# Two transformer blocks on one core: routing by token tiles with two more weight slots, a reordered second mixer, and a final norm by tiles

## The chip, the cores and the metric

The kernel runs on 1 core of one Trainium2 chip. The metric is device time in microseconds (us) for one execution; the figure for a kernel is the median of several. All data are float32. The program is written for each engine by hand: TensorE (PE) multiplies matrices into eight banks of PSUM (128 partitions x 512 floats each), VectorE (DVE), ScalarE (ACT) and GpSimd (POOL) compute on SBUF and PSUM, SyncE (SP) issues nearly all DMA loads. Engines wait for one another on semaphores only.

## The reference

256 tokens of width 1024 pass through two blocks.

```python
# block 1
h = rms_norm(x, norm1_w) @ w_in
x = x + concat(dilated_attention(q, k, v), hgrn2(...)) @ w_out
h = rms_norm(x, norm2_w)
affinity = softmax(h @ w_router)               # 16 experts
# each expert takes the 32 tokens with its highest affinity
x = x + sum over experts of affinity * down(silu(gate(h_e)) * up(h_e))   # 1024 -> 1024 -> 1024
# block 2
proj = x @ w_in_2
merged = (sigmoid(g0) * (rwkv7(...) @ w_up_rwkv) + sigmoid(g1) * (attention(q, k, v) @ w_up_moba)
          + sigmoid(g2) * (s5_with_glu(u) @ w_up_ssm))
x = layer_norm(1.189 * x + merged @ w_out_2, ln1_w, ln1_b)
x = layer_norm(1.189 * x + moe(x), ln2_w, ln2_b)  # 32 experts of 256, two for each token
```

Block 1's expert weights are 16 x 3 matrices of 4 MB: 201 MB of the 375 MB that the kernel moves. hgrn2 is a gated recurrence in both directions, s5 a state space scan, rwkv7 a recurrence with a 64 x 64 state for each of 8 heads.

## The kernel before

The work is cut into stages, each with a program for each engine. On an engine stages follow one another in the order in which the last lines of the kernel call them; where two stages alternate, a string names whose turn it is (`take_turns`, line 151), each letter being one step up to the next `yield`. A step of `project` (line 410) is half a job: 8 products of 128 x 128 by 128 x 512, or their equal.

**Slots.** Weights pass through a ring of six slots of 2 MB (`slot_number`, line 314). SyncE may load into a slot when the counter `units_used`, which TensorE raises, says that its last content has been read. For block 2 three of the slots remain (0 to 2), and the other three hold activations.

**Routing of block 1.** `out_proj1` multiplies the mixer's output by w_out, four jobs (two column halves, within each two token tiles), and VectorE adds each to x. Then, for both tiles together: `norm2` (ScalarE squares the rows, lines 349 to 362), `turn2` (TensorE turns h, line 375, VectorE copies it with norm2_w, line 388), the router's logits (line 883), softmax, the search for the 32 best of each expert (lines 936 to 942, VectorE, 16 partitions), the one-hot matrix `chosen` (line 945), and the gather of all 16 experts' tokens as a product with `chosen` (line 900), 512 columns wide. The affinities times `chosen` are turned too (lines 906, 911), for the sum over experts at the end.

**Experts of block 1.** `experts1` is a hardware loop of 4 rounds over 4 experts. An expert's inputs and the affinities are first copied by VectorE into fixed places, since the loop's matmuls need fixed addresses. Gate and up (line 1015) are products with 32 columns of weights loaded into the array, for two column strips (n = 0, 1) in turn; then hidden rows are turned (1024), multiplied by down (1035), and every four experts are added to x (1049). SyncE issues the 96 loads of 2 MB at line 998. Beside the experts, ScalarE loads the tables of the state space scan, and GpSimd works on them; both begin when the gather is over.

**Mixer of block 2.** The scan (`ssm`, line 1249) has 8 groups: drive (TensorE, line 1277), rotation and scan (VectorE, 1325 to 1336), products (GpSimd, 1364 to 1367), emit (TensorE, 1290: 8 products of 32 output columns, which take turns by output tile). TensorE alternates it with the projection for rwkv7. Then come two steps of the attention's projection, the GLU projection, and the recurrence, which alternates with the attention's and the gates' projection: this one has a single PSUM bank (7), which ScalarE must copy out (line 1245) before the next job. ScalarE also issues the loads for the recurrence (lines 1459 to 1461). The recurrence inverts matrices in doubling rounds (1563), then passes through four chunks (1592 to 1608), one after the other. After it come the rest of the gates' projections alternating with the attention, and only then `merge` (1786): for each of 8 tiles of the width the three branches' products, then VectorE's gates and sums. The output weights are the next thing in the ring, and `load_ln_rows` asks for the second router's vectors and weights when the merge is over.

**End.** The 32 experts of block 2 accumulate into four PSUM banks, which four products with zeros have opened. Then VectorE adds 1.189 x over the whole width (line 2361), `layer_norm` (1825 to 1856) goes over both tiles at once, and one store of 1 MB follows (line 2371).

## Time and profile before

| | |
|---|---|
| median of 3 runs | 1559.55 us (1558.82 to 1563.98) |
| the profiled execution | 1559.29 us, its span in the trace 1557.5 us |
| mean granted TensorE clock | 0.924 |
| TensorE busy | 1328.4 us, 85% |
| VectorE, ScalarE, GpSimd busy | 28%, 13%, 8% |
| DMA | 375.39 MB, mean 241 GB/s |

The stages by TensorE's time: block 1's projections, attention and hgrn2 to 224, output projection to 254, norm and routing to 299, its experts to 762, projection and scan to 877, GLU and the recurrence's front to 1036, its chunks to 1080, gates and attention to 1175, merge to 1220, output projection and routing 2 to 1295, experts of block 2 to 1537, norm and store to 1557. In a row of the windows, the count in brackets is the number of instructions, PEclk is the granted TensorE clock as a share of full speed, and the DMA share is that of 16 engines. Each product in the code shows as two matmul instructions in the trace.

### The profile page before, as it was taken

To read this page: it belongs to the slowest core of one execution; us is meant where nothing else is said; L and a number is where in the kernel's file an instruction comes from. 1 tells how busy PE (TensorE), PEld (TensorE's weight loads), DVE (VectorE), ACT (ScalarE), POOL (GpSimd) and SP (SyncE) were. 2 spreads that over 40 slices of the span, in tenths; PEclk is the share of its full clock that TensorE was granted. 3 is DMA by queue.
4 is the path that set the end of the run, shared out by engine and by line. 5 is a ranking of instruction groups with operands and counts; after the bars stand their busy time and mean duration, and the time that the engine had idled before them with its cause. 6 is when DMAs were issued, how large, how long until landed. Compare 5 with 4: busy or idle time off the path is not lost.

```text
span 1557.5 us, 16762 instructions
## 1 busy us (share of the span) xinstructions
PE 1328.4 (85%) x6962; PEld 678.7 (44%) x6962; DVE 440.7 (28%) x850; ACT 205.6 (13%) x372; POOL 118.1 (8%) x146
## 2 busy tenths in 40 slices
PE   6999257798997998988889888978999779999994
PEld 3574244332322322322534545867767544334341
DVE  3242752300100100100156337433442251111113
ACT  2022311000000000000000012101123013112111
POOL 0000000388000000000043200000000000000000
PEclk9999568899999999999999999995998979999998
DMA  9533102299999999999621353110230664999990
GB/s 351 210 109 113 51 0 108 86 424 428 428 427 430 427 428 430 428 428 430 243 79 57 108 189 109 56 56 1 109 108 0 251 246 174 422 421 422 421 403 28
DMA packets 62361, 375.39 MB, mean 241 GB/s; under 512 B 6112, under 2 KB 7392, under 8 KB 37472
## 3 DMA queue, kind: packets, MB, share of 16 engines
q1 hardware_dynamic: 58816, 367.87, 58.1%
q10 hardware_dynamic: 3488, 6.72, 1.2%
q8 instruction: 41, 0.67, 0.2%
q14 instruction: 16, 0.13, 0.0%
HBM read 373.53 MB, written 1.05 MB: 240 GB/s over the span
## 4 chain that ended last, share of the span: by engine, by line
PE 65%; DMA 20%; DVE 9%; ACT 3%; issue 2%; POOL 1%; SPq 0%; ACTq 0%; POOLq 0%; DVEq 0%; PEldq 0%
DMA arena<-in_w_expert_up 15%; PE psum L435 11%; PE psum L438 10%; PE psum L1015 8%; PE psum L2237 6%; DMA arena<-in_expert_w_up 3%; PE psum L1035 3%; PE psum L2261 3%; PE psum L1786 3%; PE psum L2272 2%; PE psum L1563 2%; PE psum L1888 2%; PE psum L1290 2%; PE psum L1024 1%; DVE arena L762 1%
## 5 line engine op out<-in xcount | busy, mean ns | idle before, releaser
L1015 PE MATMUL psum<-arena 128*32 128x512 f32 x1024 | 239.9, 598 | 28.8 <-DMA arena<-in_w_expert_up 22.3
L435 PE MATMUL psum<-arena 128*128 128x512 f32 x416 | 189.7, 608 | 9.5 <-ACT arena L1245 4.7
L438 PE MATMUL psum<-arena 128*128 128x256 f32 x736 | 168.2, 384 | 5.0 <-DVE arena L386 1.6
L438 PEld LDWEIGHTS psum<-arena 128*128 128x128 f32 x736 | 138.5, 191 | 30.9 <-issue 8.3
L1015 PEld LDWEIGHTS psum<-arena 128*32 128x32 f32 x1024 | 62.6, 110 | 194.4 <-issue 140.8
L1035 PE MATMUL psum<-arena 128*32 128x512 f32 x512 | 133.0, 680 | 7.6 <-ACT arena L1059 7.6
L435 PEld LDWEIGHTS psum<-arena 128*128 128x128 f32 x416 | 78.5, 194 | 108.1 <-issue 106.9
L2237 PE MATMUL psum<-arena 128*64 128x512 f32 x512 | 116.1, 595 | 1.7 <-DMA arena<-in_expert_w_up 1.4
L1077 DVE TENSOR_TENSOR arena<-arena,psum 64x512 f32<-64x512 f32 x16 | 10.9, 680 | 251.6 <-ACT arena L1057 251.6
L1035 PEld LDWEIGHTS psum<-arena 128*32 128x32 f32 x512 | 31.7, 123 | 95.9 <-issue 85.4
L2237 PEld LDWEIGHTS psum<-arena 128*64 128x64 f32 x512 | 38.2, 137 | 66.5 <-issue 66.0
L2272 PE MATMUL psum<-arena 128*128 128x512 f32 x128 | 59.3, 605 | 0.9 <-DVE arena L2348 0.9
L2261 PE MATMUL psum<-arena 128*64 128x512 f32 x256 | 57.9, 592 | 0.8 <-ACT arena L2305 0.8
L1179 POOL TENSOR_TENSOR arena<-arena 128x16 f32<-128x16 f32 (+6 forms) x64 | 43.9, 687 | 24.0 <-DMA arena<-in_ssm_bc 19.1
L1024 PE MATMUL psum<-arena 64*128 64x64 f32 x128 | 33.3, 401 | 13.6 <-DVE arena L1080 13.6
L1786 PE MATMUL psum<-arena 128*128 128x256 f32 x192 | 44.0, 394 | 0.6 <-DVE arena L607 0.6
L1364 POOL TENSOR_TENSOR arena<-arena 128x512 f32<-128x512 f32 x8 | 10.1, 1266 | 448.8 <-DVE arena L1336 405.8
L1080 DVE TENSOR_TENSOR arena<-arena,psum 64x512 f32<-64x512 f32 x16 | 10.9, 680 | 116.4 <-PE psum L1015 116.4
L1024 PEld LDWEIGHTS psum<-arena 64*128 64x128 f32 x128 | 31.0, 324 | 28.2 <-DVE arena L1080 28.2
L1786 PEld LDWEIGHTS psum<-arena 128*128 128x128 f32 x192 | 38.1, 199 | 6.9 <-issue 1.4
L1057 ACT ACTIVATE arena<-psum 64x512 f32<-64x512 f32 x16 | 9.5, 591 | 226.0 <-PE psum L1015 226.0
L2272 PEld LDWEIGHTS psum<-arena 128*128 128x128 f32 x128 | 23.0, 189 | 37.0 <-issue 35.3
(450 smaller groups left out, 1303.3 us busy)
## 6 DMA issues: line engine op xcount, KB each, us to landing
arena<-in_w_expert_gate SPq DMA_DIRECT2D x32, 2048.0 KB, 23.2
arena<-in_w_expert_up SPq DMA_DIRECT2D x32, 2048.0 KB, 24.1
arena<-in_w_expert_down SPq DMA_DIRECT2D x32, 2048.0 KB, 21.8
arena<-in_w_in SPq DMA_DIRECT2D x21, 2048.0 KB, 11.6
arena<-in_expert_w_gate SPq DMA_DIRECT2D x32, 1024.0 KB, 11.5
arena<-in_expert_w_up SPq DMA_DIRECT2D x32, 1024.0 KB, 13.6
arena<-in_expert_w_down SPq DMA_DIRECT2D x32, 1024.0 KB, 10.2
arena<-in_w_out SPq DMA_DIRECT2D x4, 2048.0 KB, 8.4
```

The lines of the kernel that those rows point to most:

```text
L435: mm = pe.matmul(o, lhs[:, k, sub * P:(sub + 1) * P], w[:, k, :], start=(k == 0), stop=(k == kt - 1))
L438: mm = pe.matmul(o, w[:, k, c:c + P], lhs[:, k, :], start=(k == 0), stop=(k == kt - 1))
L1015: mm = pe.matmul(ps[32 * n:32 * n + 32], xcur[:, k], w, start=(k == 0), stop=(k == KD - 1))
L1024: mm = pe.matmul(turned_ps[:, 64 * c:64 * c + 64], by_four[:, c], ident[0:64, 0:64], start=True, stop=True)
L1035: mm = pe.matmul(y_ps[at:at + 32, 512 * n:512 * n + 512], hid_T4[:, j, half], w_slot(e4, 4 + half)[:, j, 512 * n:512 * n + 512], start=(ha ...
L1179: mul = lambda o, a, b: step(pool.tensor_tensor(o, a, b, ALU.mult))
L1290: mm = pe.matmul(o, c[:, 32 * tile:32 * tile + 32], pr[:, n, i * SEQ:(i + 1) * SEQ], start=(n == 0), stop=(n == 3))
L1563: mm = pe.matmul(bank(b0 + t)[R, g * 64:(g + 1) * 64], lhs[R, t, g], rhs[R, t, g], start=True, stop=True)
L1786: mm = pe.matmul(o, w[:, k, d * P:(d + 1) * P], y[:, k], start=(k == 0), stop=(k == 3))
L2237: mm = pe.matmul(in_ps[ROOM * h:ROOM * (h + 1)].rearrange("p (j n) -> p j n", j=2), tokens[u % 2][:, k, ROOM * h:ROOM * (h + 1)], w_in[2 * ...
L2261: mm = pe.matmul(y_ps[ROOM * h:ROOM * (h + 1), 512 * n:512 * (n + 1)], turned[u % 2][:, f * P + ROOM * h:f * P + ROOM * (h + 1)], w_down[2 ...
L2272: mm = pe.matmul(bank(2 * t + n), turned[u % 2][:, (2 + t) * P:(3 + t) * P], y_sb[:, 512 * n:512 * (n + 1)], start=False, stop=not follows)
```

## The change

There are four parts.

1. **Routing by token tiles, two more slots.** One stage, `out_and_route`, takes the place of `out_proj1`, `norm2`, `turn2` and `route`. The output projection goes by token tile. Raw x is turned instead of the normed rows: VectorE multiplies the router's weights by norm2_w once, and the root mean square comes in as the scale of the exponential. Only the tokens of the first four experts are gathered before the experts start; the gather of the other twelve stands in experts 0 to 2, turning of the affinities in expert 3, from where on the tables' load and GpSimd's work begin. Slots 6 and 7 take up two of the first eight loads of expert weights, once; then six are used as before. The experts' loop is written out, and the copies to fixed places are gone.
2. **Block 2's mixer reordered.** Emit goes through both tiles at each of its four steps. The orders are new: two projection steps more ahead of the first emit, three projection steps instead of two ahead of the GLU, single steps in the gaps of the doubling rounds and of the chunks (which are now cut into three). The products of k and v in a chunk go ahead of the state's. ScalarE applies the gates' sigmoid as it copies out the bank. All gate projections use bank 7. The merge goes by branch, 12 jobs, and alternates with the attention; its weights come in the order ssm, rwkv, attention, each slot being free after its four jobs. ScalarE copies q and k of the attention and y of the recurrence. Block 2's slots are 3 to 5.
3. **Final norm by tiles** (`Finish`). 1.189 times the identity in place of the zeros puts 1.189 x into the banks. The statistics are taken from PSUM by tile with bn_stats, the rest goes by half rows, with four stores of 256 KB.
4. **Block 2's norm and experts.** `load_ln_rows` and the output projection wait for 4 double tiles instead of 8 tiles, and the experts' first two loads change places.

```diff
+        E1_SLOTS = [4, 5, 0, 1, 2, 3, 6, 7]
...
+                project_out(0, 0, range(KD))
+                project_out(0, 1, range(KD))
+                project_out(1, 0, range(4))
+                turn(0, 0)
+                turn(0, 1)
+                project_out(1, 0, range(4, KD))
+                route(0, range(KD))
+                project_out(1, 1, range(6))
+                turn(1, 0)
+                project_out(1, 1, range(6, KD))
+                route(1, range(2))
+                pe.wait_ge(*count("o1_product", 4))
+                pe.sem_inc(inc("units_used"), 1)
+                turn(1, 1)
+                route(1, range(2, 4))
+                route(1, range(4, KD))
...
+                for half in range(2):
+                    for j in range(4):
+                        gather(pe, 4 * half + j, bank(2 + half)[:, j * P:(j + 1) * P], slice(0, first))
...
+            beside = {0: range(0, 3), 1: range(3, 6), 2: range(6, KD)}
...
+                        before = [v for v in range(u) if slot_number(v) == slot_number(u)]
+                        if before:
+                            sp.wait_ge(*count("units_used", before[-1] + 1))
...
-                    for i in range(2):
-                        tile = 2 * s + i
-                        o = bank(4 + q % 2)[32 * (tile % 4):32 * (tile % 4) + 32, 0:SEQ]
-                        for n, c in enumerate((c_re, nc_re, nc_im, nc_im)):
+                    for n, c in enumerate((c_re, nc_re, nc_im, nc_im)):
+                        for i in range(2):
+                            tile = 2 * s + i
+                            o = bank(4 + q % 2)[32 * (tile % 4):32 * (tile % 4) + 32, 0:SEQ]
...
+            branches = ((2, ycT, ("glu_out", 1)), (0, yaT, ("rw_out", 2)), (1, ybT, ("mb_out", 4)))
+            jobs = [(place, b, y, ready, j) for place, (b, y, ready) in enumerate(branches) for j in range(KD // 2)]
...
-            act.wait_ge(*count("mg_T", KD))
+            act.wait_ge(*count("mg_T", KD // 2))
...
+                    for n in range(2):
+                        c = slice(512 * n, 512 * n + 512)
+                        dve.scalar_tensor_tensor(x_sb[:, t, c], bank(2 * t + n), self.mean_var[t][:, 0:1], ln_rows["ln2_w"][:, c],
+                                                 ALU.subtract, ALU.mult).then_inc(inc("l2_scaled"), 1)
...
-            take_turns(pe, "b" + "ab" * 16, proj_rkv.parts[0], ssm_scan.parts[0])
...
+            take_turns(pe, "baaba" + "ab" * 14, a=proj_rkv.parts[0], b=ssm_scan.parts[0])
+
+            for _ in range(3):
+                next(beside_rwkv)
             glu_proj.tensor(pe)
-            take_turns(pe, "aaaaabaaabaaaabaabaabababb" + "baaaa", lambda pe: beside_rwkv, rwkv7.parts[0])
-            take_turns(pe, ORDER2[0], proj_gates.parts[0], attention2.parts[0])
-            merged.tensor(pe)
+            take_turns(pe, "gggggr" + "gggr" + "ggggr" + "gr" * 5 + "r" + "gr" * 11 + "ggggg" + "t" + "mm" + "t" + "r" + "tm" * 14,
+                       g=lambda pe: beside_rwkv, r=rwkv7.parts[0], t=attention2.parts[0], m=merged.parts[0])
...
+            take_turns(dve, "mt" * 8 + "t", m=merged.parts[1], t=attention2.parts[1])
```

## Rows read from the trace of the kernel before

**Rows 1.** Windows: us, busy (instructions) of PE PEld DVE ACT POOL, PEclk, DMA, GB/s

```profile
19.00:63.00 44.00, 43.47 (x96) 18.95 (x96) 8.99 (x43) 1.93 (x5) 0.00 (x0) 1.00 0.85 313
...
270.00:279.00 9.00, 0.99 (x4) 0.39 (x4) 7.09 (x20) 0.26 (x3) 0.00 (x0) 0.50 0.00 0
...
299.00:762.00 463.00, 409.63 (x1702) 129.99 (x1703) 39.30 (x72) 24.41 (x40) 74.15 (x106) 0.95 1.00 422
780.00:877.00 97.00, 86.29 (x327) 41.12 (x327) 53.99 (x84) 4.18 (x7) 40.35 (x32) 0.95 0.29 98
1036.00:1080.00 44.00, 34.10 (x538) 32.20 (x534) 11.39 (x25) 4.14 (x7) 0.00 (x0) 0.67 0.01 2
1080.00:1221.00 141.00, 131.34 (x573) 103.79 (x572) 57.66 (x92) 30.37 (x74) 0.00 (x0) 0.92 0.17 60
1153.00:1175.00 22.00, 16.81 (x55) 8.50 (x54) 10.12 (x19) 9.79 (x25) 0.00 (x0) 0.73 0.26 95
```

**Rows 2.** Chain of waits, output projection to experts: start, us, what

```profile
253.90 0.70 DVE arena L847
...
263.88 5.50 PE psum L883 x32
...
271.37 0.42 DVE arena L936
...
279.09 15.73 PE psum L900 x32
...
296.57 2.43 issue
```

**Rows 3.** Timeline, SyncE and TensorE, experts 1: start, duration, instructions, [idle before <-releaser]

```profile
304.52 4.59 SPq L998 DMA_DIRECT2D arena<-in_w_expert_gate  x2
...
377.39 3.63 PE L1015 MATMUL psum<-arena 128*32 128x512 f32 x16 [0.50 <-DMA arena<-in_w_expert_gate]
...
739.59 3.63 PE L1015 MATMUL psum<-arena 128*32 128x512 f32 x16 [1.27 <-DMA arena<-in_w_expert_up]
```

**Rows 4.** Timeline, TensorE in the state space scan

```profile
795.67 5.34 PE L1290 MATMUL psum<-arena 128*32 128x256 f32 x16 [3.97 <-POOL arena L1367]
...
809.48 2.81 PE L1290 MATMUL psum<-arena 128*32 128x256 f32 x16
812.22 3.70 PE L435 MATMUL psum<-arena 128*128 128x512 f32 x8
...
873.13 4.43 PE L1290 MATMUL psum<-arena 128*32 128x256 f32 x16 [5.12 <-POOL arena L1367]
```

**Rows 5.** Timeline, front of the recurrence

```profile
902.71 4.18 ACTq L1459 DMA_DIRECT2D arena<-in_rows  x8
...
908.96 7.11 PE L435 MATMUL psum<-arena 128*128 128x512 f32 x16 [3.11 <-ACT arena L1245]
...
1029.99 3.62 PE L1563 MATMUL psum<-arena 64*64 64x64 f32 x64 [3.66 <-DVE arena L1710]
```

**Rows 6.** Timeline, chunks of the recurrence and the attention's last heads

```profile
1040.40 1.15 PE L1592 MATMUL psum<-arena 64*64 64x64 f32 x32 [1.72 <-DVE arena L1715]
...
1058.92 1.97 PE L1592 MATMUL psum<-arena 64*64 64x64 f32 x32 [1.57 <-DVE arena L1732]
...
1161.76 0.66 PE L553 MATMUL psum<-arena 128*128 128x128 f32 x4 [0.62 <-DVE arena L597]
```

**Rows 7.** Timeline, output projection of block 2

```profile
1227.75 8.96 PE L1888 MATMUL psum<-arena 128*128 128x512 f32 x16 [8.14 <-DMA arena<-in_w_out]
...
1233.49 0.46 DVE L1950 TENSOR_TENSOR arena<-arena 128x288 f32<-128x288 f32 x1 [11.14 <-DMA arena<-in_vectors]
```

**Rows 8.** Timeline of the end, and the list of DMA issues: KB, us to landing

```profile
1533.55 3.71 PE L2272 MATMUL psum<-arena 128*128 128x512 f32 x8 [0.85 <-DVE arena L2348]
...
1553.10 0.40 SPq L2371 DMA_DIRECT2D out<-arena  x1
...
out<-arena SPq DMA_DIRECT2D x1, 1024.0 KB, 4.0
```

More of the change, by code:

```diff
@@ new lines, in turn, with route @@
+                def turn(t, half):
+                    pe.wait_ge(*count("o1_out0", 2 * t + half + 1))
+                    if (t, half) == (1, 1):
+                        pe.wait_ge(*count("n2_T", 1))
+                    for j in range(4):
+                        mm = pe.transpose(turned[2 * t + half][:, j * P:(j + 1) * P],
+                                          x_sb[:, t, (4 * half + j) * P:(4 * half + j + 1) * P], ident)
+                    mm.then_inc(inc("n2_turned"), 1)
+                def route(t, ks):
+                    pe.wait_ge(*count("n2_T", 2 * t + ks[-1] // 4 + 1))
+                    for k in ks:
+                        mm = pe.matmul(logits[t], x2_T[:, k, t * P:(t + 1) * P], wr[:, k], start=(k == 0), stop=(k == KD - 1))
+                    if ks[-1] == KD - 1:
+                        mm.then_inc(inc("r_logits"), 1)
@@ new lines, in gather, with gather_other @@
+            def gather(pe, k, o, slots):
+                for t in range(NT):
+                    by_four = h2[:, t].rearrange("p (h q j) -> p h j q", h=2, j=4)
+                    mm = pe.matmul(o, by_four[:, k // 4, k % 4], by_tile[:, t, slots], start=(t == 0), stop=(t == NT - 1))
+                if slots.start or k % 4 == 3:
+                    mm.then_inc(inc("r_gathered"), 1)
+            def gather_other(pe, k):
+                if k == 0:
+                    pe.wait_ge(*count("r_chosen", 2))
+                if k >= 2:
+                    pe.wait_ge(*count("r_xin", 2 + k - 1))
+                gather(pe, k, bank(6 + k % 2)[:, 0:others], slice(first, NSLOT))
@@ L930, in vector, with add_out, copy_turned @@
-                dve.tensor_reduce(nmax, logits, AXX, ALU.max, negate=True).then_inc(inc("r_max"), 1)
+                def add_out(t, c):
+                    dve.wait_ge(*count("o1_product", 2 * t + c + 1))
+                    part = x_sb[:, t, 512 * c:512 * (c + 1)]
+                    dve.tensor_tensor(part, part, bank(2 * t + c), ALU.add).then_inc(inc("o1_out0"), 1)
+                def copy_turned(t, half):
+                    dve.wait_ge(*count("n2_turned", 2 * t + half + 1))
+                    dve.tensor_copy(x2_T[:, 4 * half:4 * half + 4, t * P:(t + 1) * P],
+                                    turned[2 * t + half].rearrange("p (k s) -> p k s", k=4)).then_inc(inc("n2_T"), 1)
@@ L1811, in merge @@
-            return Stage(tensor=tensor, vector=vector, scalar=scalar)
+                for i, (place, b, y, ready, j) in enumerate(jobs):
+                    two_tiles = slice(2 * j, 2 * j + 2)
+                    g = g3[:, b, two_tiles]
+                    dve.wait_ge(*count("mg_products", i + 1))
+                    dve.tensor_tensor(g, g, bank(2 + i % 2).rearrange("p (e s) -> p e s", e=2), ALU.mult)\
+                       .then_inc(inc("mg_out"), 1)
+                    dve.wait_ge(*count("mg_out", i + 1))
+                    if place == 1:
+                        dve.tensor_tensor(g, g, g3[:, 2, two_tiles], ALU.add).then_inc(inc("mg_two"), 1)
+                    if place == 2:
+                        dve.wait_ge(*count("mg_two", j + 1))
+                        dve.tensor_tensor(mergedT[:, two_tiles], g, g3[:, 0, two_tiles], ALU.add).then_inc(inc("mg_T"), 1)
+                    yield
@@ L2359, in vector @@
                 either(dve, loop)
-                xf = x_sb.rearrange("p t d -> p (t d)")
-                dve.scalar_tensor_tensor(xf, xf, DEEPNORM_ALPHA, banks(0, 4), ALU.mult, ALU.add).then_inc(inc("m2_added"), 1)
+                for t in range(NT):
+                    dve.wait_ge(*count("m2_combined", t + 1))
+                    finish.statistics(dve, t)
+                finish.rows(dve)
             cols.release("m2_y")
```

671 lines of the change are left out of this document (383 added, 288 removed), and 4 rows, old and new, of the table SHARED.

## The prediction

> **What bounds the kernel now.** I read the windows by stage first [rows 1] (columns in the group's line). TensorE is busy for 85 to 99% of most stages, so it is the bound of block 1's front and of block 2; the experts of block 1 are different. In 299 to 762 the DMA share is 1.00 at 422 GB/s: 96 half matrices of 2 MB pass through six slots, and TensorE waits again and again for one, the first time at 377.39 and the last at 739.59 [rows 3]. Between the two lie 75 loads, 362.2 / 75 = 4.83 us each. So this stage ends when its last loads land, whatever TensorE does.
>
> Ahead of it the chain of waits shows what holds the stream back [rows 2]: the last add of the output projection at 253.90, then norm, transposes and copies until the logits start at 263.88, softmax, top-k on VectorE from 271.37 on, 15.73 us of gather, and 2.43 us until the first expert's matmul at 299.00. The next load is issued only at 304.52 [rows 3]. In the recurrence of 1036 to 1080 TensorE is busy 34.10 of 44 us, but at a granted clock of 0.67 [rows 1]: the same 32 matmuls take 1.15 us at 1040.40 and 1.97 us at 1058.92 [rows 6]. The attention tail (1153 to 1175) has 0.73. Near the end an output weight is waited for, 8.14 us before 1227.75 [rows 7], and the final norm runs alone, from the last matmul at 1537.26 to the store at 1553.10 [rows 8].
>
> **Part 1, routing and first experts.** The output projection keeps its place, with its products by token tile, so tile 0's square sum, transposes and logits lie beside tile 1's products. Three of four transpose groups and 18 of 32 router matmuls now stand between the products, some 3.5 us (0.17 us for a router matmul at the low clock of before, 5.50 / 32 [rows 2], half of that here), so the last product ends near 257.6 (before 253.9, with 0.3 for the wait on the weighted router). After it come one add, two half-row squares, one turn and 4 of the 8 router steps: 3.8 us, to 261.4, where before the logits ended at 269.38 [rows 2]. From the logits to the gather all stays as long as before, 279.09 - 269.38 = 9.7, less 0.6 for a comparison of 4 experts instead of 16: 270.5. The gather shrinks from 512 columns to the 128 of four experts for the wait: 32 matmuls at a quarter of the columns, 15.73 / 4 = 3.9 us at full speed; 7 at the low clock, which I take since in 270 to 279 TensorE was busy 0.99 of 9 us and the clock was 0.50 [rows 1]. First expert at 278, 21 us earlier. If the gather is warm 24, if each new hand-over costs 0.5 us more, 17.
>
> The two extra slots take two loads (9.7 us) out of the stream. They are consumed once, and while expert 1 reads them no load can be issued: the eighth next load waits for unit 8 of the experts. With the other experts' gather (8 x 4 matmuls of 384 columns, about 10 us) spread over experts 0 to 2, I count 7 us of DMA idle in the first 55 us. Against that the ramp of before cost 10 (304.52 to 377.39 for 13 loads, 72.9 against 62.8) and is partly the same time. Laid out load by load, the wait of the last gate/up half comes 432 us after the first expert's start, 8.4 sooner than the 440.6 of before. Bounds: nothing, and 9.7. TensorE alone would need about 412 to the same place (409.63 busy [rows 1], 22 of it behind that wait, 10 more for the gather, and 1 us of hand-over in each of 16 experts), so DMA stays the bound, by 20 us. Moved with this: the tables' load on ScalarE's queue and GpSimd's table work, which begin after expert 3, some 80 us later; GpSimd was busy 74.15 us in this window [rows 1] and now has 300. **Part 1: -29 us.**
>
> The experts' loop is written out, about 200 TensorE instructions for each expert. In 19 to 63 straight code ran beside a DMA share of 0.85 and TensorE stood still for 0.5 us [rows 1]; so I price it at nothing. The Trainium skill (Runtime: NRT & Kernel Launch, Instruction fetch mechanics) says that a taken branch breaks the sequential prefetch and can stall. By that rule three back edges of TensorE's loop would go and the change gain a little more; the sum takes nothing for it, since DMA is the bound there.
>
> **Part 2, state space scan.** Its 8 groups of 16 output matmuls take 2.81 us each [rows 4], 0.17 us a matmul; a 512-column one takes 3.70 / 8, so 256 columns want 0.22 if nothing overlaps. The new order alternates the two column strips at every step. The experts' matmuls alternate strips in the same way, and at 3.63 / 16 = 0.23 us for 512 columns [rows 3] they cost half of that 0.46. So 1.8 us a group, gain 8 x 1.0 = 8. Two more projection steps stand ahead of the first group, where TensorE idled 3.97 and then ran 2.5 us too long (5.34 against 2.81) [rows 4]: gain 6.5. These steps are missing at the end, where the last two groups now wait for GpSimd one after the other: idle of 5 and 5.3 where it was 5.12 before the last, and a cold last group as before. 8 + 6.5 - 5.2 is 9.3, and 0.7 for that last group, cold only once: the scan ends at 867.5 instead of 877.5: **-10** (from -2, if the strips already overlapped, to -12).
>
> **Part 3, start of the recurrence.** ScalarE must now issue ten loads (eight of them took 4.18 us [rows 5]) and do the lora activations before it copies job 2 out of the single bank 7. Before, TensorE waited 3.11 us for that copy [rows 5], because job 2 lay wholly behind the GLU projection; now half of it is done early, so the wait begins one step, 3.6, earlier and ends 0.9 later: 3.11 + 4.5 = 7.6, and a cold start of 3. That is +7.5. The step itself is only moved. In the doubling rounds each gap has one step instead of two, one or none: the first gap is short by 3.3, the last saves the 3.66 wait [rows 5] and 1.5 of cold clock; -2. Together **+5.5** (0 to +10).
>
> **Part 4, recurrence, gates, attention, merge** (1036.0 to VectorE's last merge instruction at 1233.49 - 11.14 = 1222.3 [rows 7], 186.3 us). The TensorE work at full clock: 34.10 x 0.67 = 23 and 131.34 x 0.92 = 121 [rows 1]. It stays. What can go are 42 us of idle time and low clock. Eleven of the 16 gate steps (3.6 each) now fill the gaps of the four chunks, of 1.72 or 1.57 [rows 6]: nearly all of 44 - 23 = 21 us goes there. What stays or comes: 1.7 ahead of the first state product, 3 for the single bank, 5 at the first softmax, 2 at the end. And a new one: VectorE takes a merge product, then the division of the next head. The merge product of job h+1 is only ready after TensorE's last step ahead of turn h+1, so that turn waits for a multiply of 0.7, a reciprocal of 0.17, a multiply of 0.7 and two hand-overs, 1.9; from job 4 an add more, 2.6. Before, it waited 0.62 [rows 6]. 3 x 1.9 + 4 x 2.6 = 16. So 144 + 28, and 3 for small hand-overs, is 175: **-11**. The stretch of before that had such waits, 1153 to 1175, ran at 0.73 [rows 1]. I add 5 us for low clock that comes and goes: **-6** (-20 to +45).
>
> **Part 5, output weights.** The 8.14 us wait goes, since the first weight loads during the attention and the second during the last merge jobs. But the next is late at once: the second router's column vectors, asked for only when the merge is done, gave VectorE its operands at 1233.49, 11.1 us after its last merge instruction [rows 7], and TensorE's first projection (16 matmuls, 7.1 us warm as in [rows 5]) will be over sooner. With VectorE's own work on them it then waits some 5 and runs on cold. Of 8 us I keep **-1** (-4 to +1).
>
> **Part 6, the end.** Alpha x rides on the four matmuls that cleared the banks. After the last matmul (1533.55 + 3.71 = 1537.26 [rows 8]): tile 1's statistics 1.9, root 0.5, then four halves of two VectorE instructions, 0.7 each and a hand-over, 5.8: 1545.6. The last 0.25 MB store takes 2 to 4 us by the 4.0 of 1 MB [rows 8]. End at about 1548.8: **-8.7** (-7.5 to -9.5). The expert loop of block 2 begins with the other pair loaded first; both land long before it starts: nothing.
>
> Sum: -29 - 10 + 5.5 - 6 - 1 - 8.7 = -49. The profiled execution took 1559.29 us (span 1557.5), the median is 1559.55: 1559.3 - 49.2, **1510 us**.
>
> **Rivals.**
> A. The stream starts earlier but gains no more: TensorE's added gather and the slots used once leave DMA idle as long as the two loads are worth. For it: six outstanding slots again from expert 2 on; against it: the share was 1.00 over the whole window [rows 1], while TensorE stood still for 53 us of it. 1510 + 9 = 1519.
> B. The output matmuls gain nothing by their order. 2.81 is already less than 16 x 0.22 = 3.5. 1510 + 8 = 1518.
> C. The other side: the clock falls at the 5 us wait of the first softmax and stays down, as it did between 1040 and 1058 [rows 6] and to 1080 (0.67 [rows 1]). Attention, y transposes and the merge (about 58 us at full clock from there) then take twice as long. Against it: those matmuls filled a quarter of the array, and merge steps, which fill it, stand between; 1080 to 1221 with such steps had 0.92 [rows 1]. Price +54 over the forecast's own allowance of 5: 1510 + 53 = 1563. It decides the sign once more than 50 us of work runs at half speed. The Trainium skill (TensorE: Matmul & The Clock Gate, Part 1) calls the low clock the default that only activity lifts.
> D. The bounds fall well: warm gather, short hand-overs, warm attention: 1495.
>
> **How the numbers follow.** The forecast 0.58 (1500 to 1518), A or B 0.18 (1514 to 1530), D 0.14, C whole 0.04, C in part 0.06 (1530 to 1556). Leaving out C and half of what is below 1495: 1491 to 1532. A measurement tells 0.3% (4.7 us) from no change. Slower 0.04, same 0.02, faster 0.94.
>
> **What would show it.** First expert matmul near 278; next load near 283; last wait for an up half near 710. Groups of 16 output matmuls at 1.7. A wait of about 8 for ScalarE after the GLU. The chunks with gate steps between and a clock over 0.95; waits of 2 to 2.6 for VectorE ahead of each turned head; a wait for the router vectors in place of the output weight; 11 us from the last matmul to the end. The prediction is wrong if the clock stays low in the attention, or if the DMA share in the experts is below 0.97.

## The result: 18 us faster, not 49

| | median, us | runs |
|---|---|---|
| before | 1559.42 | 1558.82 to 1563.98, 4 runs |
| changed | 1541.03 | 1535.46 to 1543.15, 4 runs |

The medians lie 18.4 us apart. The ratio of the two kernels is 0.9863, 95% interval 0.9842 to 0.9885, which is 21 us less, 18 to 25 by its bounds. The forecast was 1510 with a range of 1491 to 1532, so the sign was right and the size far off. The profiled execution took 1543.15 us (span 1541.4), 16.1 less than the span of before. It is the slowest of the four, 2.1 above their median.

Where the two traces part can be told from marks that both have. The lead is the time of before less the time of the changed kernel; the last two columns say what each stage added to it.

| mark | before | changed | lead | stage gave | forecast |
|---|---|---|---|---|---|
| first expert's matmul | 299.00 | 277.61 | 21.4 | +21.4 | +21 |
| last wait for an up half | 739.59 | 721.34 | 18.3 | -3.1 | +8.4 |
| end of the last emit | 877.49 | 851.29 | 26.2 | +7.9 | +10 |
| start of the chunks' first product | 1036.65 | 1021.37 | 15.3 | -10.9 | -5.5 |
| VectorE's wait for the second router's vectors begins | 1222.35 | 1207.95 | 14.4 | -0.9 | +6 |
| last matmul, its end | 1537.26 | 1530.95 | 6.3 | -8.1 | +1 |
| end of the span | 1557.5 | 1541.4 | 16.1 | +9.8 | +8.7 |

Two steps of the forecast hold, to half a us (the start of the experts) and to 1 us (the end); five lie between 2 and 12 us beside it, all to the same side.

The windows of the changed kernel by stage (columns as in [rows 1]):

```profile
281.00:310.00 29.00, 28.52 (x120) 11.47 (x117) 3.21 (x5) 0.98 (x2) 0.00 (x0) 0.94 0.91 361
310.00:330.00 20.00, 19.52 (x82) 9.21 (x81) 4.35 (x6) 0.98 (x2) 2.38 (x4) 1.00 0.75 274
330.00:340.00 10.00, 10.00 (x54) 2.98 (x51) 0.00 (x0) 0.00 (x0) 0.00 (x0) 1.00 1.00 398
340.00:380.00 40.00, 39.05 (x169) 15.80 (x166) 3.96 (x6) 3.53 (x7) 0.00 (x0) 0.96 1.01 429
400.00:720.00 320.00, 278.96 (x1178) 86.72 (x1174) 21.14 (x31) 13.40 (x25) 73.58 (x106) 0.96 1.01 428
...
1021.00:1207.00 186.00, 160.28 (x1100) 127.53 (x1094) 62.29 (x105) 32.18 (x74) 0.00 (x0) 0.93 0.20 73
...
1207.00:1243.00 36.00, 23.22 (x58) 11.95 (x59) 5.08 (x16) 1.49 (x2) 0.00 (x0) 0.76 0.63 246
```

The first three rows show the stream of expert weights below its later rate of 428 GB/s, 310 to 330 at 274 GB/s. The kernel before has no such hole: it moves 344 GB/s in its first 30 us (299 to 329) and 429 in the next 28. Over the whole stage, 277.6 to 741, the DMA share is 0.98.

The row of 1021 to 1207 is as long as the same stretch of the kernel before:

```profile
1036.00:1222.00 186.00, 165.44 (x1108) 135.99 (x1104) 69.96 (x121) 34.51 (x81) 0.00 (x0) 0.86 0.13 47
```

The clock rose from 0.86 to 0.93, and TensorE stands idle for 25.7 us instead of 20.6. The row of 1207 to 1243 is the output projection, with TensorE idle for 12.8 us of 36 and at 0.76.

TensorE's timeline names the waits, in the order of the table's losses (columns as in [rows 3]):

```profile
721.34 3.63 PE L1168 MATMUL psum<-arena 128*32 128x512 f32 x16 [1.27 <-DMA arena<-in_w_expert_up]
...
831.36 1.92 PE L1442 MATMUL psum<-arena 128*32 128x256 f32 x16
...
839.39 3.21 PE L1442 MATMUL psum<-arena 128*32 128x256 f32 x16 [5.05 <-POOL arena L1519]
847.73 3.63 PE L1442 MATMUL psum<-arena 128*32 128x256 f32 x16 [5.13 <-POOL arena L1519]
...
888.84 9.29 PE L443 MATMUL psum<-arena 128*128 128x512 f32 x16 [7.86 <-ACT arena L1560]
...
969.20 3.68 PE L1729 MATMUL psum<-arena 64*64 64x64 f32 x64 [3.11 <-DVE arena L1876]
974.00 6.00 PE L1729 MATMUL psum<-arena 64*64 64x64 f32 x128 [1.12 <-ACT arena L1647]
...
1131.46 0.66 PE L561 MATMUL psum<-arena 128*128 128x128 f32 x4 [1.71 <-DVE arena L608]
...
1156.31 1.12 PE L561 MATMUL psum<-arena 128*128 128x128 f32 x4 [2.31 <-DVE arena L608]
1157.22 3.01 PE L1960 MATMUL psum<-arena 128*128 128x256 f32 x8
...
1226.91 3.69 PE L2094 MATMUL psum<-arena 128*128 128x72 f32 x16 [12.54 <-DVE arena L2130]
```

(Below, cold is said of matmuls that ran at the lower of the clock's two levels, 0.50 in the windows, and warm of those at full clock.) The waits of 1.71 stand ahead of heads 1 to 3 and those of 2.31 ahead of heads 4 to 7. The merge products behind the first three of 2.31 take 3.01 to 3.03 us, where those behind a 1.71 take 1.89. And the wait of 12.54 us is not for an output weight, as 8.14 in [rows 7] was, but for VectorE, which waits for the second router's vectors:

```profile
1226.03 0.46 DVE L2129 TENSOR_TENSOR arena<-arena 128x288 f32<-128x288 f32 x1 [18.08 <-DMA arena<-in_vectors]
```

The end is as forecast. The last matmul ends at 1530.95, the store of four quarters begins at 1534.40, and from the last matmul to the end of the span pass 10.4 us (20.2 before):

```profile
1532.84 0.75 DVE L2363 SCALAR_TENSOR_TENSOR arena<-psum,arena 128x512 f32<-128x512 f32 x1
...
1534.40 4.88 SPq L2594 DMA_DIRECT2D out<-arena  x4
```

### The profile page after: what moved, and what is told of

Same layout as the page of the kernel before. It is cut to its first block, busy times and chain, and to the rows that moved or that the text cites. A ratio compares the mean times of both kernels' runs of the same rounds, so it can differ in the third digit from the quotient of the medians.

```text
span 1541.4 us, 16435 instructions
## 1 busy us (share of the span) xinstructions
PE 1316.7 (85%) x6994; PEld 670.9 (44%) x6994; DVE 424.2 (28%) x823; ACT 202.9 (13%) x372; POOL 116.5 (8%) x146
## 4 chain that ended last, share of the span: by engine, by line
PE 68%; DMA 18%; DVE 8%; ACT 3%; issue 1%; POOL 1%; ACTq 0%; SPq 0%; POOLq 0%; DVEq 0%
DMA arena<-in_w_expert_up 12%; PE psum L446 10%; PE psum L443 10%; PE psum L1168 9%; PE psum L2456 6%; PE psum L1196 4%; DMA arena<-in_expert_w_up 3%; PE psum L1960 3%; PE psum L2480 3%; PE psum L2491 2%; PE psum L1729 2%; PE psum L898 2%; PE psum L2067 1%; PE psum L1184 1%; PE psum L958 1%; DMA arena<-in_vectors 1%
## 5 line engine op out<-in xcount | busy, mean ns | idle before, releaser
L1168 PE MATMUL psum<-arena 128*32 128x512 f32 x1024 | 235.7, 594 | 25.4 <-DMA arena<-in_w_expert_up 19.5
L446 PE MATMUL psum<-arena 128*128 128x256 f32 x736 | 170.0, 386 | 6.3 <-ACT arena L1562 3.1
L443 PE MATMUL psum<-arena 128*128 128x512 f32 x352 | 161.9, 611 | 13.9 <-ACT arena L1560 10.2
L446 PEld LDWEIGHTS psum<-arena 128*128 128x128 f32 x736 | 138.2, 191 | 32.1 <-issue 10.0
L1196 PE MATMUL psum<-arena 128*32 128x512 f32 x512 | 129.4, 664 | 7.6 <-ACT arena L1215 7.6
L443 PEld LDWEIGHTS psum<-arena 128*128 128x128 f32 x352 | 66.3, 195 | 98.1 <-issue 98.1
L1226 DVE TENSOR_TENSOR arena<-arena,psum 64x512 f32<-64x512 f32 x16 | 10.9, 680 | 251.4 <-ACT arena L1210 251.4
L2491 PE MATMUL psum<-arena 128*128 128x512 f32 x128 | 59.3, 605 | 0.9 <-DVE arena L2569 0.9
L1960 PE MATMUL psum<-arena 128*128 128x256 f32 x192 | 51.6, 425 | 0.6 <-issue 0.6
L1960 PEld LDWEIGHTS psum<-arena 128*128 128x128 f32 x192 | 40.4, 218 | 9.7 <-issue 3.7
L1229 DVE TENSOR_TENSOR arena<-arena,psum 64x512 f32<-64x512 f32 x16 | 10.9, 680 | 112.7 <-PE psum L1168 112.7
L1729 PE MATMUL psum<-arena 64*64 64x64 f32 x896 | 31.9, 234 | 8.9 <-ACT arena L1647 5.6
L2491 PEld LDWEIGHTS psum<-arena 128*128 128x128 f32 x128 | 23.0, 189 | 37.0 <-issue 35.3
## 6 DMA issues: line engine op xcount, KB each, us to landing
arena<-in_expert_w_gate SPq DMA_DIRECT2D x32, 1024.0 KB, 11.5
```

The costliest lines, as they stand in the source:

```text
L443: mm = pe.matmul(o, lhs[:, k, sub * P:(sub + 1) * P], w[:, k, :], start=(k == 0), stop=(k == kt - 1))
L446: mm = pe.matmul(o, w[:, k, c:c + P], lhs[:, k, :], start=(k == 0), stop=(k == kt - 1))
L1168: mm = pe.matmul(ps[32 * n:32 * n + 32], xin[:, e, k], w[:, j, 512 * n:512 * n + 512], start=(k == 0), stop=(k == KD - 1))
L1196: mm = pe.matmul(y_ps[at:at + 32, 512 * n:512 * n + 512], hid_T4[:, j, half], w[:, j, 512 * n:512 * n + 512], start=(half == 0 and j == 0) ...
L1729: mm = pe.matmul(bank(b0 + t)[R, g * 64:(g + 1) * 64], lhs[R, t, g], rhs[R, t, g], start=True, stop=True)
L1960: mm = pe.matmul(bank(2 + i % 2)[:, e * SEQ:(e + 1) * SEQ], w[:, k, d * P:(d + 1) * P], y[:, k], start=(k == 0), stop=(k == 3))
```

## The experiments

All are edits of the changed kernel, the last two on top of four other edits, timed beside the kernel before on the same chip. Since they ran on other chips than the changed kernel itself, the ratio to before is what is compared with 0.9863, and the gains given in us are these differences of ratios times 1560.

### e1_hold: block 2's expert loads wait for the router's vectors

```diff
             def sync(sp):
-                sp.wait_ge(*count("mg_T", KD // 2))
+                sp.wait_ge(*count("late_loaded", 32))
                 load(sp, 0, 0)
```

> Against the changed kernel: SyncE's loads of block 2's expert weights wait until the second router's weights and vectors have landed. Theory (they are late because six loads of 1 MB issued in the same 2 us share the DMA engines with them, 17.9 us to landing against 11.0 before): they land within 9 us of the last merge, TensorE's wait of 12.54 us ahead of the router's column sums falls to 2 to 4, its two cold groups are warm, and the time falls by 9 to 12 us, to about 1530. Rival (the time to landing is that of 1024 small rows, whatever runs beside them): the wait stays over 10 us and the time is unchanged.

Measured: 1526.63 us, ratio 0.9776 (0.9755 to 0.9798), some 14 us less. The list of DMA issues from 1200 on, in the changed kernel and then here (KB, us to landing):

```profile
arena<-in_expert_w_gate SPq DMA_DIRECT2D x2, 1024.0 KB, 7.2
...
arena<-in_w_router ACTq DMA_DIRECT2D x1, 144.0 KB, 17.9
arena<-in_vectors ACTq DMA_DIRECT2D x1, 16.0 KB, 18.3
```

```profile
arena<-in_expert_w_gate SPq DMA_DIRECT2D x2, 1024.0 KB, 12.2
...
arena<-in_w_router ACTq DMA_DIRECT2D x1, 144.0 KB, 2.5
arena<-in_vectors ACTq DMA_DIRECT2D x1, 16.0 KB, 2.5
```

Without those loads beside them they land in 2.5 us, where up to 9 had been expected. In the changed kernel SyncE issued six loads of 1 MB in the same 3 us, and they landed first, within 7.2 to 14.9 us. TensorE no longer waits there, and from the first output product to the gather of block 2 pass 48.4 us instead of 65.0, with a granted clock of 1.00 up to 1245. The rival is out.

### e2_copy: ScalarE copies job 1 before it issues the ten loads

```diff
-            take_turns(act, "rr" + "ggg" + "r" + ...
+            take_turns(act, "grr" + "gg" + "r" + ...
```

> Against the changed kernel: ScalarE copies job 1 out of bank 7 before it issues the ten loads and does the lora activations, not behind them. Theory (TensorE's wait of 7.86 us after the GLU projection, and the cold 9.29 us behind it, are lost time): the wait falls to under 1 us and the recurrence's chunks begin 7 to 9 us sooner; time about 1532. Rival (the front of the recurrence is a chain on VectorE, which these 8 us of TensorE do not shorten): the wait goes, but TensorE waits as much longer ahead of the doubling rounds, and the time stays within 2 us.

Measured: 1526.19 us, ratio 0.9778 (0.9759 to 0.9796), 13 us less, more than expected. TensorE's timeline here:

```profile
876.33 3.67 PE L443 MATMUL psum<-arena 128*128 128x512 f32 x8
880.78 7.10 PE L443 MATMUL psum<-arena 128*128 128x512 f32 x16 [0.78 <-ACT arena L1560]
...
957.38 3.31 PE L1729 MATMUL psum<-arena 64*64 64x64 f32 x64 [3.11 <-DVE arena L1876]
961.82 3.95 PE L1729 MATMUL psum<-arena 64*64 64x64 f32 x128 [1.13 <-ACT arena L1647]
```

The wait is 0.78 instead of 7.86, the job behind it takes 7.10 instead of 9.29. From the last emit's end to the chunks pass 156.4 us instead of 170.1: 7.1 of the 13.7 are the wait, 2.2 the cold job, and the rest are in the main products of the inversion which are faster here (3.95 at 961.82, 6.00 in the changed kernel). This last part is not all the edit's: in the kernels that leave this front alone it takes 165.7 to 170.3 us. The rival, a chain on VectorE that would take the gain away, is out.

### e3_divide: VectorE divides before it takes the merge product

```diff
-            take_turns(dve, "mt" * 8 + "t", m=merged.parts[1], t=attention2.parts[1])
+            take_turns(dve, "mt" + "tm" * 7 + "t", m=merged.parts[1], t=attention2.parts[1])
```

> Against the changed kernel: in the attention VectorE divides head h+1 before it takes the merge product of job h+1, so that the division no longer stands behind a product that comes last. Theory (the waits of 1.71 and 2.31 us ahead of each turned head are this order): they fall under 0.5 us, 12 us in all, and with them the clock no longer drops, so 13 to 18 us are gained; time about 1526. Rival (the chain from scores through bias, exponential and division is as long as a head's matmuls, 6.7 us): the waits shrink by less than half.

Measured: 1519.30 us, ratio 0.9733 (0.9713 to 0.9752), 20 us less.

```profile
1124.27 1.11 PE L561 MATMUL psum<-arena 128*128 128x128 f32 x4 [4.07 <-DVE arena L608]
...
1133.39 0.60 PE L561 MATMUL psum<-arena 128*128 128x128 f32 x4
...
1158.01 0.60 PE L561 MATMUL psum<-arena 128*128 128x128 f32 x4
```

Ahead of heads 1 to 7 there is no wait at all. The stretch that took 186 us takes 161:

```profile
1026.00:1187.00 161.00, 149.56 (x1098) 120.87 (x1093) 62.14 (x104) 31.48 (x74) 0.00 (x0) 0.98 0.23 85
```

The seven waits were 3 x 1.71 + 4 x 2.31 = 14.4 us. The other 10.7 of the 25 are TensorE's busy time, 149.56 us instead of 160.28: the same products at a higher clock, 0.98 for 0.93.

### e4_six: the old six slots

```diff
-        E1_SLOTS = [4, 5, 0, 1, 2, 3, 6, 7]
+        E1_SLOTS = [4, 5, 0, 1, 2, 3]
```

> Against the changed kernel: block 1's expert loads use the six old slots only, the rest of the routing is as changed. By the prediction the two extra slots take 9.7 us of loads out of the stream and cost 1.3, so without them the last wait for an up half comes 8 us later (about 729) and the time is 1549. Theory after the result (slots used once leave the DMA engines idle through the first half of expert 1, some 16 us in bytes against 6): with six slots the stream runs without that hole, 88 loads of 4.91 us from 281.3 on, so the last wait comes at about 717, 4 us sooner, and the time is 1537.

Measured: 1544.92 us, ratio 0.9903 (0.9886 to 0.9920), 6 us more. Neither number was met: the last wait comes at 723.80, 446.2 us after the first expert's start instead of 443.7. The two extra slots gain 2.5 us in the trace, not 8.4 and not -4. (Five other kernels with the same slots and routing, e1, e2, e3, e6 and e7, have 441.8 to 443.7, so the gain can be up to 4.4.) The windows show why it is so little:

```profile
281.00:310.00 29.00, 28.53 (x120) 11.46 (x117) 3.21 (x5) 0.97 (x2) 0.00 (x0) 0.94 0.92 361
310.00:330.00 20.00, 19.53 (x82) 9.22 (x81) 4.35 (x6) 0.97 (x2) 2.39 (x4) 1.00 1.00 413
330.00:340.00 10.00, 10.00 (x54) 2.97 (x51) 0.00 (x0) 0.00 (x0) 0.00 (x0) 1.00 1.01 431
```

In 310 to 330 the stream now moves 413 GB/s instead of 274, and in 330 to 340 431 instead of 398. These differences are 6.5 and 0.8 us at 428, and the two loads that the slots take out are worth 2 x 4.9. What is left, 9.8 - 7.3 = 2.5 us, is what they gave. What else of the 6 us in the time is due to them and what to the clock, which differs from run to run in the attention, is open.

### e5_twice: slot 6 used a second time

```diff
-        E1_SLOTS = [4, 5, 0, 1, 2, 3, 6, 7]
+        E1_SLOTS = [4, 5, 0, 1, 2, 3, 6, 7, 4, 5, 0, 1, 2, 3, 6]
```

> Against the changed kernel: slot 6 is used a second time (for the 15th load, an up half of expert 2) and slot 7 once. Theory (the hole in the stream during the first half of expert 1, 310 to 330 at 262 and 285 GB/s, is there because the slots that expert 1 gives back are not loaded again): the stream gets one load ahead there and the last wait for an up half comes 4 to 5 us sooner, 439 us after the first expert's start instead of 443.7; time about 1537. Rival (the gather in experts 0 to 2 holds the loads back, not the slots): less than 1.5 us.

Measured: 1538.60 us, ratio 0.9866 (0.9826 to 0.9906), no difference; the last wait comes 443.1 us after the start, 0.6 sooner and within the spread of the kernels without the edit (441.8 to 443.7). The windows show where the load ahead went:

```profile
310.00:330.00 20.00, 19.52 (x82) 9.29 (x81) 4.35 (x6) 0.98 (x2) 2.39 (x4) 1.00 0.94 378
...
340.00:380.00 40.00, 39.05 (x168) 15.89 (x167) 3.96 (x6) 3.53 (x7) 0.00 (x0) 0.96 0.95 388
```

Two thirds of the hole are closed (378 instead of 274 GB/s, one load of 2 MB), and a new one opens in 340 to 380 (388 instead of 429). The load that the stream was ahead is given back before expert 4. My theory fell, and the rival's number came true: something holds the stream in experts 0 to 3 that more slots at one place don't lift. In the three later kernels with this edit the wait comes after 442.3, 438.9 and 443.4 us, so only one of the four stands clear of that spread.

### e10_half: half of the late gather left out

The gather for the twelve other experts leaves out the second token tile, so these experts get only part of their tokens.

```diff
-                gather(pe, k, bank(6 + k % 2)[:, 0:others], slice(first, NSLOT))
+                by_four = h2[:, 0].rearrange("p (h q j) -> p h j q", h=2, j=4)
+                mm = pe.matmul(bank(6 + k % 2)[:, 0:others], by_four[:, k // 4, k % 4], by_tile[:, 0, first:NSLOT],
+                               start=True, stop=True)
```

> Against the changed kernel: the gather of the other twelve experts in experts 0 to 2 leaves out the second tile's tokens (half of its matmuls, 5.7 us of TensorE). Theory (with six slots the stream can be no further ahead than TensorE's pace in experts 0 to 3 lets it, so these experts and not the DMA engines set when the last load is asked for): expert 4 begins 5.7 us sooner and the last wait for an up half 4 to 6 us sooner, about 438 us after the first expert's start. Rival (the prediction's: the DMA engines are the bound by 20 us over the whole stage): under 1.5 us.

Measured: 1537.68 us, ratio 0.9841 (0.9816 to 0.9866). The gather costs 7.2 us instead of 11.5, expert 4 begins 112.3 us after the first expert instead of 115.5, and the last wait comes after 441.5 instead of 443.7.

```profile
319.57 2.78 PE L969 MATMUL psum<-arena 128*128 128x384 f32 x6
...
390.65 4.92 PE L1171 MATMUL psum<-arena 128*32 128x512 f32 x22
...
719.89 3.63 PE L1171 MATMUL psum<-arena 128*32 128x512 f32 x16 [1.27 <-DMA arena<-in_w_expert_up]
```

TensorE is 3.2 us faster up to expert 4, and the last wait comes 2.2 sooner. But the kernels without this edit have 441.8 to 443.7, so 441.5 does not stand clear of them, and the run decides no further than this: the 4 to 6 us of the theory are not met. How the hole comes about is argued, not shown. In the changed kernel TensorE takes 28.9 us for each of experts 0 to 3 (115.5 / 4), and six loads take 29.4 at 4.90 each. So it gives slots back about as fast as the stream fills them, and a stream that starts two loads ahead must wait for it. From 400 on the stream runs at 428 GB/s.

### e6_emit: the emit in its old order

```diff
-                    for n, c in enumerate((c_re, nc_re, nc_im, nc_im)):
-                        for i in range(2):
+                    for i in range(2):
+                        for n, c in enumerate((c_re, nc_re, nc_im, nc_im)):
```

(The two assignments between the loops stay in the loop over i.)

> Against the changed kernel: the emit of the state space scan in its old order, tile by tile, everything else as changed. Theory (the order halves no more than the part that did not overlap, 2.81 to 1.92 us a group in the traces): the scan is 6 to 7 us longer, time about 1547. Rival (the scan's end is set by GpSimd's products, so that the order of emit is hidden): 2 us or less.

Measured: 1545.90 us, ratio 0.9910 (0.9875 to 0.9945), 7 us more, as the theory says. In the trace the stretch from the transposes at 742.38 to the end of the last emit takes 119.8 us, against 108.3 in the changed kernel. Of these 11.5 us the emits are 9: 0.89 us in each of six warm groups, and 2.05 and 1.56 in the two cold ones. Half a us comes back in a shorter wait (4.52), and 3 us are a cold start ahead of the first emit (9.35 us for a projection job of 7.13), which the edit does not touch.

```profile
838.29 2.78 PE L1442 MATMUL psum<-arena 128*32 128x256 f32 x16
846.65 5.26 PE L1442 MATMUL psum<-arena 128*32 128x256 f32 x16 [4.52 <-POOL arena L1519]
857.03 5.19 PE L1442 MATMUL psum<-arena 128*32 128x256 f32 x16 [5.12 <-POOL arena L1519]
```

### e7_lead: TensorE one merge job ahead

```diff
-                       ... + "ggggg" + "t" + "mm" + "t" + "r" + "tm" * 14,
+                       ... + "ggggg" + "t" + "mm" + "t" + "r" + "mm" + "tm" * 12,
```

> Against the changed kernel: TensorE does merge job 1 ahead of the first turned head, and so is one merge job ahead of the attention's heads from there on; VectorE's order is as changed (merge product, then division). Theory (VectorE is late because the product it takes first is TensorE's latest): the waits of 1.71 and 2.31 us ahead of the turned heads go as in the kernel with the division first, and the 4.07 us ahead of the first one nearly too; 20 to 26 us less than the changed kernel, time about 1518. Rival (the order on VectorE itself costs the time): as the changed kernel, less 4 us.

Measured: 1512.09 us, ratio 0.9685 (0.9648 to 0.9722), 28 us less than the changed kernel, 7 more than the division first gave. VectorE's order is the same as in the changed kernel, and the waits are gone all the same:

```profile
1106.11 1.94 PE L539 MATMUL psum<-arena 128*128 128x128 f32 x16 [1.02 <-ACT arena L1562]
1117.66 0.66 PE L561 MATMUL psum<-arena 128*128 128x128 f32 x4 [0.62 <-DVE arena L608]
1155.94 1.08 PE L574 MATMUL psum<-arena 128*64 128x256 f32 x4 [0.69 <-ACT arena L642]
...
1020.00:1176.00 156.00, 146.73 (x1098) 119.06 (x1094) 62.43 (x105) 31.47 (x74) 0.00 (x0) 1.00 0.25 88
```

The first three rows are every wait of TensorE between 1106 and 1156; the only one ahead of a turned head is 0.62, where it was 4.07. The last row is the window of the stretch, 156 us at a clock of 1.00. So VectorE's order costs nothing when the product that it takes first is there early. The waits need both, a late product and a division that stands behind it: moving either takes them away (e3_divide, e7_lead). The lead takes away the 4.07 as well, which the order does not.

### e8_all: e1, e2, e5 and e7 at once

> Four edits at once on the changed kernel: block 2's expert loads held back, ScalarE's copy first, one merge job ahead, slot 6 used twice. If the four losses are separate, their gains add up: 14 + 15 + 22 + 4 = 55 us, time about 1486. If they share a cause (the clock after an idle stretch), it is 1500 or more.

Measured: 1485.85 us, ratio 0.9515 (0.9478 to 0.9553), 54 us less than the changed kernel. One by one the edits gave 14, 13, 28 and nothing, so three losses add up: they were separate. That the expected 1486 was met is partly luck, since it took 22 for the lead and 4 for the slot.

### e9_order: one step moved into the first doubling gap

```diff
-            ... "gggggr" + "gggr" + "ggggr" + "gr" * 5 + "r"
+            ... "ggggr" + "gggr" + "ggggr" + "ggr" + "gr" * 4 + "r"
```

> Against the kernel with all four edits (1485.85 us): one projection step is taken from the five ahead of the recurrence's front and put into the gap of the first doubling round, where TensorE waits 3.11 us for VectorE and then runs cold. Theory (the prediction's: this gap is short by one step): the wait goes and 3 to 4 us are gained, about 1482. Rival (the front is a chain on VectorE and the step is needed ahead of it): as much new waiting ahead of the lora products, and the time stays within 1 us.

Measured: 1484.90 us, ratio 0.9503 (0.9472 to 0.9533), no difference. The wait of 3.11 is gone, and two others are there, which the kernel with four edits does not have:

```profile
901.95 1.98 PE L1679 MATMUL psum<-arena 128*128 128x512 f32 x4 [0.54 <-DVE arena L1812]
...
935.42 4.15 PE L1698 MATMUL psum<-arena 128*128 128x128 f32 x32 [1.86 <-DVE arena L1846]
```

With the late copy mended, the chain on VectorE is the next thing in line. The rival was right: the front takes 156.5 us instead of 157.1.

### e11_fill: two projection steps in the scan's last gaps

On top of the four edits:

```diff
-            take_turns(pe, "baaba" + "ab" * 14, a=proj_rkv.parts[0], b=ssm_scan.parts[0])
-
-            for _ in range(3):
-                next(beside_rwkv)
+            programs = {"a": proj_rkv.parts[0](pe), "b": ssm_scan.parts[0](pe), "c": beside_rwkv}
+            for which in "baaba" + "ab" * 11 + "bcbbcb" + "aabbc":
+                next(programs[which], None)
...
+            copies_beside = proj_qkv2.parts[1](act)
+            next(copies_beside)
             ssm_scan.scalar(act)
-            copies_beside = proj_qkv2.parts[1](act)
-            next(copies_beside)
```

> Against the kernel with all four edits (1485.85 us): two of the three projection steps that follow the state space scan stand in its last two gaps instead, where TensorE waits 5.05 and 5.14 us for GpSimd and runs the emit cold (3.42 and 3.63 us against 1.92). ScalarE copies their job ahead of the gelu's sigmoid. Theory: the idle time shrinks by 7 us, 2 to 3 us come back as a wait for the gelu, and both emits are warm: 6 to 9 us less, about 1478. Rival (the GLU projection starts when the gelu is ready, which these steps do not move): 2 us or less.

Measured: 1480.02 us, ratio 0.9476 (0.9434 to 0.9518). The interval overlaps that of e8_all, so the times alone don't settle the 6 us between them; the trace shows a gain: from the transposes ahead of the scan to the GLU projection pass 114.2 us instead of 123.8. In the changed kernel and e2_copy, which leave this stretch alone as well, it takes 120.2, so the edit's own part is 6 to 10 us.

```profile
834.11 3.70 PE L443 MATMUL psum<-arena 128*128 128x512 f32 x8
839.25 1.92 PE L1442 MATMUL psum<-arena 128*32 128x256 f32 x16 [1.44 <-POOL arena L1519]
841.10 3.70 PE L443 MATMUL psum<-arena 128*128 128x512 f32 x8
847.28 1.92 PE L1442 MATMUL psum<-arena 128*32 128x256 f32 x16 [2.48 <-POOL arena L1519]
849.13 3.70 PE L443 MATMUL psum<-arena 128*128 128x512 f32 x8
855.37 9.94 PE L446 MATMUL psum<-arena 128*128 128x256 f32 x37 [2.55 <-DVE arena L1502]
```

Both emits are warm, and 2.55 us come back as the wait for the gelu. This version is 80 us faster than the kernel before.

## Why the prediction was wrong

**Start of the experts (forecast -21).** Right: first matmul at 277.61 for a forecast of 278, next load at 281.27 for 283. The gather of four experts began at 269.42 for 270.5 and took 8.13 us for an assumed 7, so two misses of 1.1 us cancel. The clock was low as assumed for the first 5 us of it (0.50 in 269 to 274, 1.00 from 276 on).

**Two slots, laid out load by load (forecast -8.4).** This step failed by 11.5 us (443.7 us for a forecast of 432), by two terms of its sum. The DMA idle time was put at 7 us; 59 us at 338 GB/s (281 to 340) are 12.4 us of idle at 428, five more. And a load was taken at 4.83 us, where 2 MB at 428 GB/s take 4.90: 86 loads make 6 us of that. This was a counting mistake. The wait at 377.39 is for the second gate half of expert 3, the last one for the second up half of expert 15, and between them lie 74 loads, not 75: 362.2 / 74 = 4.895 us, the stream's own rate. By the same mistake the ramp of the kernel before is 14 loads, not 13, and cost some 4 us where the prediction has 10. Two further terms were put at nothing or too high: the tables of the scan, 1 MB, were loaded at 296.67 in the kernel before, when nothing else was loading, and are loaded at 387.71 in the changed one, inside the full stream, by an estimate 2.4 us at 428 GB/s; and the next load follows the first expert's start by 3.7 us for 5. The mechanism, that slots used once leave a hole while expert 1 reads them, was right (e4_six). "DMA stays the bound, by 20 us" was right for the stage as a whole (share 0.98, so the sign of being wrong, a share under 0.97, did not come) and no guide to its first quarter, where the stream also waits for TensorE to give slots back. Rival A comes nearest: by e4_six the slots gained 2.5 us.

**Scan (forecast -10).** Right in its mechanism: groups of 1.92 us for 1.8, waits of 5.05 and 5.13 for 5 and 5.3. The last two groups were both cold (3.21 and 3.63), not one; it gave 7.9. Undoing the order costs what it should (e6_emit), so rival B is out.

**Start of the recurrence (forecast +5.5).** The wait was 7.86 for a forecast of 7.6 and its cold job 2.2 for 3. What was missed is that nothing came back: the step "first gap short by 3.3, last saves 3.66" held (3.11 and none), but the inversion's products ran partly at the low clock, 5.84 and 6.00 us at two places. It cost 10.9, and one letter in ScalarE's order gives 13.7 back (e2_copy). I had priced this wait and not asked whether it had to be.

**Recurrence to merge (forecast -6).** The new waits were right in place and nearly in size: 14.4 us for 16, and 4.07 for 5 at the first softmax. The work at full clock was put at 144 us, and is 146.8 (e8_all, clock 1.00). TensorE was idle for 25.7 us and lost another 13.5 to the clock (186 - 25.7 - 146.8), where I had put 31 and 5 for the two. The term that failed is the 5 us for the clock. Part of the 13.5 is this one execution: four other kernels that leave this stretch alone (e4, e5, e6, e10) take 181.2 to 181.5 us, not 186, mostly because the products behind the first wait in the chunks are warm (3.73 us where the changed kernel's trace has 5.99 at 1028.58), and so is the first merge product behind a 2.31. The chunks themselves came as forecast, 0.96 in 1021 to 1110. Rival C, the clock staying down for good, did not come; its price (the prediction has 54 in one place and 53 in its sum) was far too large, but a clock that falls after the 2.31 us waits, 0.81 in 1154 to 1190, did cost what I had left to it as a part. The Trainium skill (TensorE: Matmul & The Clock Gate, Part 1) calls the low clock the default that only activity lifts; by that rule the clock rises where waits go, and the trace of e7_lead agrees, with 1.00 over 156 us.

**Output weights (forecast -1).** The step that failed outright. I took the router's vectors as arriving 11.1 us after the last merge because they had done so in [rows 7]. In the kernel before, block 2's expert loads were issued over 6 us and behind two output weights; with those out of the way early, the six loads of 1 MB started together with the vectors and the vectors came after 18.08 us. The wait was 12.54 us for "some 5", and what followed ran cold: the stage lost 8.1 us. The duration of a transfer was carried over into a place where its neighbours had changed. e1_hold shows it by the 2.5 us that the same load takes alone.

**The written-out loop (forecast 0).** The Trainium skill (Runtime: NRT & Kernel Launch, Instruction fetch mechanics) says that a taken branch can stall an engine until its instructions are fetched. No trace here shows such a gap: in the kernel before, the first expert behind the loop's back edge starts at 407.99, where the product ahead of it ends at 408.06. It played no part in the miss.

**The end (forecast -8.7).** Right, 9.8. The last quarter's store lands in 2.0 us, the lower end assumed.

In all, 11.5 + 2.1 + 5.4 + 6.9 + 9.1, less 1.1 at the end and 0.4 at the start, are the 33.5 us by which the profiled span missed the forecast. The range missed the median by 9 us: it left out that several small losses would fall to the same side. Rival D, all bounds falling well, did not come.

## What to carry to other kernels

- When an edit starts one transfer earlier, look at what will now be issued beside the small ones. A few KB that many engines wait for go ahead of megabytes that nobody needs yet.
- Where two programs alternate on two engines, let the producer be one job ahead. The consumer's order then need not be changed, and short waits disappear with it, and with them the low clock behind them. That was worth 28 us here; with the late copy and the crowded load it was 54, more than the change itself (21).
- Slots that are used once help only if what they hold back can be refilled. And check the time of one load against the bytes: 2 MB in 4.83 us would be 434 GB/s, where the window of the whole stage has 422. A rate above the measured one is a sign of a miscount.

## What the runs showed of the hardware

- A load of 144 KB in 1024 rows lands in 2.5 us with no other load ahead of it or beside it from SyncE (e1_hold), in 11.0 beside two loads of 2 MB and the first expert loads (the kernel before), and in 17.9 beside six loads of 1 MB issued within the same 3 us (the changed kernel).
- Eight products of 32 output columns (16 matmul instructions) take 2.81 us when all of one output tile come first and 1.92 us when they alternate between two tiles (e6_emit and the changed kernel).
- After waits of 5 to 12 us TensorE's next short groups took 1.7 to 1.9 times as long (3.21 and 3.63 for 1.92, 3.69 for 1.90). After waits of 1.71 us they did not (8 merge products in 1.89 us). After waits of 2.31 us they mostly did: in the changed kernel behind all four (3.01 to 3.03 for 1.89, and behind the last 1.97 for 1.08), in e4, e5, e6 and e10 behind three of four. In the same stretch without such waits the granted clock was 1.00 (e7_lead).
